# Where DVE's additions of low rows stand among its subtractions, and which engine converts the high part of the experts' activations

## The chip, the cores and the metric

One core of one Trainium2 chip runs the whole kernel in one launch. The time is device microseconds of that core; the kernel before takes 2709.88 us, the median of 3 runs (2704.93 to 2712.09).

## What is computed

Two small transformer stacks, one after the other, on 256 tokens of width 1024 in float32. The first has two layers, each a mixer (attention or a recurrence) followed by a mixture of experts; the second has attention, a long convolution and two dense blocks. The change touches the mixture of experts alone. Cut to what matters:

```python
for g in range(N_GROUPS):          # 4 groups of 8 experts, 2 experts a token
    hid = silu(einsum('nd,edf->nef', x, w_gate[g])) * einsum('nd,edf->nef', x, w_up[g])
    y = y + einsum('nef,efd->nd', hid * combine[:, g, :, None], w_down[g])
```

There are 32 experts a layer. w_gate and w_up are 1024x512 each, w_down is 512x1024: three slabs of 2 MB an expert.

## The kernel before

**Five engines with a program each.** The program is written by hand for every engine, and each engine runs its list strictly in the order in which it is written; they meet at semaphores. So what stands ahead of what on an engine is what the Python code says, and no scheduler changes it. SP issues the loads of weights, 2 MB at a time, into a ring of six slabs. PE multiplies. ACT and DVE do the rest; POOL does little.

**Two parts of every float32 number.** PE multiplies in the format fp32r, which keeps fewer bits. To keep precision, a weight w is split into a high part (w converted to fp32r) and a low part (w minus the high part). ACT makes the high part of half a slab (`make_high`, L1698, 128x2048, into one of four buffers `high`), DVE the low part (`make_low`, L2394, written over the slab in place), and PE multiplies with both. The activations are split as well: `seated2` for the gathered tokens, `hidden2` for the hidden values of an expert, whose high part stands in `hidden2[:, :, 0]` and its low part in `hidden2[:, :, 1]`. The left operand of a matmul holds the high and low parts of 64 tokens side by side in 128 rows, so a bank has 64 rows for the high and 64 for the low part, which have to be added.

**Rounds.** `moe_short` (taken when no expert has more than 64 tokens, as here) runs 16 rounds a layer, one for each pair of experts, 0 and 1. On PE a round is: gate0, up0 (L1126), then down1 of the pair before (L1153), fold0 (L1143), the turn of the routing weights, gate1, up1, the scatter of the pair before (L1174), gathers for the next pair (L1115) with down0 between them, and fold1. Names like down0.1 are expert 0, second half of the slab. Rounds 2 to 14 are one hardware loop; rounds 0, 1 and 15 are written out.

**ACT in a round** (L1739 to L1760): `into` takes one projection's result out of its bank between the two `make_high` of a later slab; `empty_rows` copies the 64 low rows of down's bank to `low_rows`; `silu(e)` and `turn_weights` and `gather` take banks out. A `make_high` may begin when PE is done with the buffer that it overwrites (semaphore `half_used` or the bank's count). The slab that each one prepares is one or two steps ahead: during gate0 it is down1, during up0 gate1, during down1 up1, during gate1 down0, during up1 gate0 of the next round, during down0 up0 of the next round (`next_weights`, L460).

**DVE in a round** (L2424 to L2443): `refill` makes the two low parts of the same slab as ACT's. `add_rows(e, half, r)` adds `low_rows` to the high rows of down's bank and frees that bank (L2421). `hide(e, r)` (L2402) waits for the fold's bank and for silu, multiplies (L2408), casts the product to fp32r as the high part (L2411), waits for that cast, and subtracts for the low part (L2413), which PE's down waits for (semaphore `hidden`). `weigh` (L2380) and `take_seats` (L2372) are four short instructions each, for the routing weights and for the places of the next tokens.

**Banks.** Four PSUM banks carry the round by a fixed table (`FILLS`). PE may fill a bank only when its last content was taken out: gate1's bank holds down1.0 before it, so PE waits there for `add_rows(1, 0)`; up1's holds down1.1; up0's holds down0.1 of the round before; gate0's holds down0.0.

Of the kernel before, what the change touches and what calls it, by code (L numbers as in the profile page):

```python
# [16 lines left out]
F32 = mybir.dt.float32  # L17
# [3 lines left out]
ALU = mybir.AluOpType  # L21
# [308 lines left out]
def build(nc, A, out):  # L330
# [5 lines left out]
    with ctx:  # L336
# [1171 lines left out]
        def _(act):  # L1508
# [177 lines left out]
            def moe_short(layer):  # L1686
# [44 lines left out]

                def gather(j, r):
                    out_of(f"gather{j}", r, seated2[:, 2 * j:2 * j + 2].rearrange("p k e a c -> p (k e a c)"),
                           lambda ps: ps[:, :])

                def turn_weights(r):
                    out_of("turn", r, weightedT, lambda ps: ps[:, 0:2 * P])

                def round_(r, first=False, last=False):  # L1739
                    into("gate0", 0, r, first, last)  # L1740
                    into("up0", 1, r, first, last)
                    if not first:
                        down(1, 0, r, first, last)
                        down(1, 1, r, first, last)
                    silu(0, r)
                    if not first:
                        turn_weights(r)
                    into("gate1", 0, r, first, last)
                    into("up1", 1, r, first, last)
                    if not last:  # L1750
                        gather(0, r)
                        gather(1, r)
                    down(0, 0, r, first, last)
                    if not last:
                        gather(2, r)
                    empty_rows(0, 1, r)
                    if not last:
                        gather(3, r)
                    refill("down0", r, 1, first, last)
                    silu(1, r)  # L1760

# [134 lines left out]
        def _(dve):  # L1896
# [470 lines left out]
            def moe_short(layer):  # L2367
# [20 lines left out]
                def make_low(name, r):  # L2388

                    for half in range(2):  # L2390
                        n, hi = weight_part(name, r, half)
                        w, low = (weight_half(layer, name, half, x) for x in (False, True))
                        dve.wait_ge(sem(f"high{layer}"), n + 1)
                        v.tensor_tensor(low, w, hi.bitcast(F32), ALU.subtract)\  # L2394
                            .then_inc(sem(f"low{layer}"), 1)

                def refill(name, r, first, last):
                    follower = next_weights(name, r, first, last)
                    if follower is not None:
                        make_low(*follower)  # L2400

                def hide(e, r):  # L2402
# [3 lines left out]
                    steps = sem(f"hide_step{layer}")  # L2406
                    h4_, s4 = (x.rearrange("p (f c) -> p f c", f=4) for x in (pair_h, pair_silu))
                    v.tensor_tensor(h4_, s4, ps[:, 4 * SEATS:8 * SEATS].rearrange("p (f c) -> p f c", f=4), ALU.mult)\  # L2408
                        .then_inc(moe_drained[layer][u.bank], 1)
                    moe_empty(dve, layer, u)  # L2410
                    v.tensor_copy(hidden2[:, :, 0], h4_).then_inc(steps, 1)  # L2411
                    dve.wait_ge(steps, r * 2 + (e + 1))
# [11 lines left out]
                def round_(r, first=False, last=False):  # L2424
                    refill("gate0", r, first, last)
                    refill("up0", r, first, last)
                    if not first:
                        add_rows(1, 0, r)
                        add_rows(1, 1, r)
                        refill("down1", r, first, last)  # L2430
# [3 lines left out]
                    weigh(r)  # L2434
                    refill("gate1", r, first, last)
                    refill("up1", r, first, last)
                    add_rows(0, 0, r)
                    add_rows(0, 1, r)
                    refill("down0", r, first, last)
# [3 lines left out]
                    hide(1, r)  # L2443
# [3 lines left out]
                make_low("gate0", 0)  # L2447
                make_low("up0", 0)
# [378 lines left out]
```

## Time and profile before

| | |
|---|---|
| median of 3 runs | 2709.88 us |
| the profiled execution | 2710.59 us |
| its span on the core | 2708.5 us |
| busy: PE, DVE, ACT | 2371.8, 1968.6, 1342.7 us |
| costliest group: the low parts of the experts' weights on DVE (L2394), 384 instructions | 856.6 us |
| next: their high parts on ACT (L1698), 384 instructions | 726.9 us |
| mean granted clock of PE | 0.928 |

A busy time is the sum of an engine's instructions, and a share is that over the whole span, in which stages with different limits follow each other; it tells which engine works most, not which one the others wait for. For that one reads a single stage in order of time, with the idle time before each instruction and what ended it.

### The profile page before, as it was taken

The page shows a single profiled execution, that of the slowest core. Times are in us where ns is not written, and L with a number is a line of the kernel's source. Part 1 is how long each engine was busy: PE and PEld are TensorE (multiplying, and loading weights), DVE is VectorE, ACT ScalarE, POOL GpSimd, SP SyncE. Part 2 cuts the span into 40 slices and gives each one's busy share as a digit, 9 for nine tenths or more (in the row PEclk, how much of TensorE's full clock was granted, in tenths as well). Part 3 has the DMA queues.
Part 4 walks back from the last instruction along what each step waited for, and adds up shares of the span by engine and source line. Part 5 has one row for each costly group of instructions (what it writes and reads, how often), then busy time and mean ns, then how long its engine had stood idle before and what let it go on. Part 6 is the DMA issues. An engine that isn't in the chain of part 4 may idle for free.

```text
span 2708.5 us, 29901 instructions
## 1 busy us (share of the span) xinstructions
PE 2371.8 (88%) x10986; PEld 1749.8 (65%) x10986; DVE 1968.6 (73%) x2443; ACT 1342.7 (50%) x1477; POOL 23.9 (1%) x45
## 2 busy tenths in 40 slices
PE   7996999999998967999999987898799568877998
PEld 6555777777773546777777764565788225733887
DVE  3737999999984548999999985447876644368775
ACT  3225888888872417888888841262432111100432
POOL 0000000000000000000000000000000000000000
PEclk9986999999998988999999997899899678988999
DMA  8313989888993215899989883304656501306370
GB/s 316 124 63 144 367 349 359 355 343 352 353 361 115 112 63 221 348 353 354 362 348 367 354 304 112 124 32 158 231 194 226 212 31 54 133 8 242 140 279 17
DMA packets 116505, 607.80 MB, mean 224 GB/s; under 512 B 5300, under 2 KB 8428, under 8 KB 91644
## 3 DMA queue, kind: packets, MB, share of 16 engines
q1 hardware_dynamic: 111536, 588.83, 56.9%
q0 software_dynamic: 4880, 17.76, 1.8%
q8 instruction: 60, 0.98, 0.2%
q14 instruction: 29, 0.24, 0.0%
HBM read 605.51 MB, written 1.05 MB: 224 GB/s over the span
## 4 chain that ended last, share of the span: by engine, by line
PE 59%; DVE 21%; issue 12%; ACT 7%; DVEq 1%; DMA 0%; POOL 0%; ACTq 0%; SPq 0%
PE bank L900 10%; PE bank L1126 9%; DVE slab_parts L2394 6%; PE bank L912 4%; PE bank L1174 4%; ACT high L1698 3%; PE bank L999 3%; PE bank L1153 3%; PE bank L1387 2%; PE bank L1389 2%; PE bank L1388 2%; PE bank L1400 2%; PE bank L1402 2%; PE bank L1401 2%; PE bank L1115 2%
## 5 line engine op out<-in xcount | busy, mean ns | idle before, releaser
L2394 DVE TENSOR_TENSOR slab_parts<-ring,high 128x2048 fp32r<-128x2048 f32 x384 | 856.6, 2285 | 18.1 <-ACT high L1698 14.2
L1698 ACT ACTIVATE high<-ring 128x2048 fp32r<-128x2048 f32 x384 | 726.9, 1911 | 94.4 <-PE bank L1126 79.9
L1126 PE MATMUL bank<-high,xT_parts 128*128 128x512 f32 x1024 | 291.9, 408 | 34.1 <-DVE arena L2421 32.7
L1126 PE MATMUL bank<-slab_parts,xT_parts 128*128 128x512 f32 x1024 | 282.2, 398 | 0.0
L1538 ACT ACTIVATE arena<-bank 128x512 f32<-128x512 f32 (+4 forms) x162 | 89.5, 586 | 361.2 <-PE bank L900 99.5
L900 PE MATMUL bank<-ring,xT 128*128 128x512 f32 (+3 forms) x576 | 240.5, 579 | 11.1 <-DVE xT L2025 7.1
L1126 PEld LDWEIGHTS bank<-high,xT_parts 128*128 128x128 f32 x1024 | 191.9, 192 | 81.7 <-DVE slab_parts L2394 34.9
L1126 PEld LDWEIGHTS bank<-slab_parts,xT_parts 128*128 128x128 f32 x1024 | 196.3, 192 | 45.8
L1690 ACT ACTIVATE arena<-bank 64x512 f32<-64x512 f32 (+2 forms) x352 | 184.4, 533 | 62.2 <-PE bank L1153 54.6
L900 PEld LDWEIGHTS bank<-ring,xT 128*128 128x128 f32 x576 | 112.1, 196 | 136.3 <-issue 124.7
L1153 PE MATMUL bank<-high,hidden_parts 128*128 128x512 f32 x512 | 151.5, 418 | 18.0 <-DVE slab_parts L2394 11.8
L1558 ACT ACTIVATE high<-ring 128x2048 fp32r<-128x2048 f32 x64 | 121.8, 1913 | 87.8 <-PE bank L1402 82.2
L2606 DVE TENSOR_TENSOR slab_parts<-ring,high 128x2048 fp32r<-128x2048 f32 x64 | 146.1, 2291 | 20.9 <-ACT high L1558 20.5
L1387 PE MATMUL bank<-xT_parts,high 128*128 128x256 f32 x512 | 148.2, 289 | 10.2 <-DVE slab_parts L2606 10.2
L1389 PE MATMUL bank<-xT_parts,slab_parts 128*128 128x256 f32 x512 | 145.7, 285 | 0.0
L1388 PE MATMUL bank<-xT_low,high 128*128 128x256 f32 x512 | 145.6, 284 | 0.0
L2421 DVE TENSOR_TENSOR arena<-arena,bank 64x512 f32<-64x512 f32 x128 | 84.6, 680 | 79.1 <-ACT arena L1690 77.3
L1153 PE MATMUL bank<-slab_parts,hidden_parts 128*128 128x512 f32 x512 | 141.9, 399 | 0.0
L1143 PEld LDWEIGHTS bank<-arena 128*128 128x128 f32 x1024 | 121.8, 192 | 5.9 <-ACT arena L1690 3.1
L1143 PE MATMUL bank<-arena 128*128 128x64 f32 x1024 | 123.0, 273 | 2.3 <-ACT arena L1690 2.3
L1153 PEld LDWEIGHTS bank<-high,hidden_parts 128*128 128x128 f32 x512 | 88.1, 191 | 56.9 <-DVE slab_parts L2394 34.5
L1115 PE MATMUL bank<-sel,u_high 128*128 128x128 f32 x512 | 109.7, 297 | 11.4 <-DVE sel L2372 7.8
(361 smaller groups left out, 3635.9 us busy)
## 6 DMA issues: line engine op xcount, KB each, us to landing
ring<-in_moe_w_gate SPq DMA_DIRECT2D x64, 2048.0 KB, 8.1
ring<-in_moe_w_up SPq DMA_DIRECT2D x64, 2048.0 KB, 10.0
ring<-in_moe_w_down SPq DMA_DIRECT2D x64, 2048.0 KB, 9.0
ring<-in_mlp_w SPq DMA_DIRECT2D x32, 2048.0 KB, 13.6
ring<-in_w_mod SPq DMA_DIRECT2D x24, 2048.0 KB, 7.9
ring<-in_even_w_in SPq DMA_DIRECT2D x7, 2048.0 KB, 21.3
ring<-in_odd_w_in SPq DMA_DIRECT2D x6, 2048.0 KB, 9.6
ring<-in_h_w_in SPq DMA_DIRECT2D x6, 2048.0 KB, 8.2
```

The source lines that it names most:

```text
L900: last = mm(banks[u.bank][:, 0:n], lhs(k, tile), w[:, k, c0:c0 + n], start=(k == 0), stop=(k == k_tiles - 1))
L1115: last = mm(dst5[:, c, :, a], u_parts[a][:, t, 2 * j + c, :], sel[:, t], start=(t == 0), stop=(t == 1))
L1126: last = mm(dst[:, :], seated2[:, 4 * half + k, e], part_[:, k, :], start=(half == a == k == 0), stop=(half == a == 1 and k == 3))
L1143: last = mm(dst[:, (4 * w + f) * SEATS:(4 * w + f + 1) * SEATS], raw[:, w, f * P:(f + 1) * P], fold, start=True, stop=True)
L1153: last = mm(dst[:, :], hidden2[:, f], part_[:, f, :], start=(a == f == 0), stop=(a == 1 and f == 3))
L1387: mm(dst, w_high[:, k, fs], xT_high[:, k, :], start=(k == 0), stop=False)
L1388: mm(dst, w_high[:, k, fs], xT_low[:, k, :], start=False, stop=False)
L1389: last = mm(dst, w_low[:, k, fs], xT_high[:, k, :], start=False, stop=(k == KD - 1))
L1690: act_fn(dst, src(banks[u.bank]), func).then_inc(done or moe_drained[layer][u.bank], 1)
L1698: act_fn(hi, weight_half(layer, name, half), ACT.Copy).then_inc(sem(f"high{layer}"), 1)
L2394: v.tensor_tensor(low, w, hi.bitcast(F32), ALU.subtract)\
L2606: v.tensor_tensor(w_low, loaded, w_high.bitcast(F32), ALU.subtract).then_inc(sem("mlp_low"), 1)
```

## The change

It does two things in `moe_short`, in every round of both layers. On DVE the two additions of an expert's low rows no longer stand next to each other: `make_low` and `refill` are cut into halves (`make_low_after`), and a subtraction of weights stands between the two additions of down1 and another between those of down0. And the high part of the hidden values is no longer a cast on DVE: ACT writes it (`hidden_high`, 128x256, from SBUF to SBUF, when the multiplication has drained the fold's bank), and DVE's last subtraction (`hide_low`) waits for ACT. The multiplication `hide` and `hide_low` are now apart, with `weigh` or `take_seats` between them; `take_seats` comes behind `hide(1)`.

```diff
@@ -1729,6 +1729,11 @@
                 def silu(e, r):
                     out_of(f"fold{e}", r, pair_silu, lambda ps: ps[:, 0:4 * SEATS], ACT.Silu, sem(f"silu{layer}"))
 
+                def hidden_high(e, r):
+                    moe_empty(act, layer, filling(f"fold{e}", r))
+                    act_fn(hidden2[:, :, 0], pair_h.rearrange("p (f c) -> p f c", f=4), ACT.Copy)\
+                        .then_inc(sem(f"hidden_high{layer}"), 1)
+
                 def gather(j, r):
                     out_of(f"gather{j}", r, seated2[:, 2 * j:2 * j + 2].rearrange("p k e a c -> p (k e a c)"),
                            lambda ps: ps[:, :])
@@ -1745,6 +1750,7 @@
                     silu(0, r)
                     if not first:
                         turn_weights(r)
+                    hidden_high(0, r)
                     into("gate1", 0, r, first, last)
                     into("up1", 1, r, first, last)
                     if not last:
@@ -1758,6 +1764,7 @@
                         gather(3, r)
                     refill("down0", r, 1, first, last)
                     silu(1, r)
+                    hidden_high(1, r)
 
                 for name in ("gate0", "up0"):
                     for half in range(2):
@@ -2385,31 +2392,34 @@
                     moe_full(dve, layer, u)
                     return u, banks[u.bank]
 
-                def make_low(name, r):
-
-                    for half in range(2):
-                        n, hi = weight_part(name, r, half)
-                        w, low = (weight_half(layer, name, half, x) for x in (False, True))
-                        dve.wait_ge(sem(f"high{layer}"), n + 1)
-                        v.tensor_tensor(low, w, hi.bitcast(F32), ALU.subtract)\
-                            .then_inc(sem(f"low{layer}"), 1)
-
-                def refill(name, r, first, last):
+                def make_low(name, r, half):
+
+                    n, hi = weight_part(name, r, half)
+                    w, low = (weight_half(layer, name, half, x) for x in (False, True))
+                    dve.wait_ge(sem(f"high{layer}"), n + 1)
+                    v.tensor_tensor(low, w, hi.bitcast(F32), ALU.subtract).then_inc(sem(f"low{layer}"), 1)
+
+                def make_low_after(name, r, half, first, last):
                     follower = next_weights(name, r, first, last)
                     if follower is not None:
-                        make_low(*follower)
+                        make_low(*follower, half)
+
+                def refill(name, r, first, last):
+                    for half in range(2):
+                        make_low_after(name, r, half, first, last)
+
+                h4_, s4 = (x.rearrange("p (f c) -> p f c", f=4) for x in (pair_h, pair_silu))
 
                 def hide(e, r):
 
                     u, ps = filled(f"fold{e}", r)
                     dve.wait_ge(sem(f"silu{layer}"), r * 2 + (e + 1))
-                    steps = sem(f"hide_step{layer}")
-                    h4_, s4 = (x.rearrange("p (f c) -> p f c", f=4) for x in (pair_h, pair_silu))
                     v.tensor_tensor(h4_, s4, ps[:, 4 * SEATS:8 * SEATS].rearrange("p (f c) -> p f c", f=4), ALU.mult)\
                         .then_inc(moe_drained[layer][u.bank], 1)
-                    moe_empty(dve, layer, u)
-                    v.tensor_copy(hidden2[:, :, 0], h4_).then_inc(steps, 1)
-                    dve.wait_ge(steps, r * 2 + (e + 1))
+
+                def hide_low(e, r):
+
+                    dve.wait_ge(sem(f"hidden_high{layer}"), r * 2 + (e + 1))
                     v.tensor_tensor(hidden2[:, :, 1], h4_, hidden2[:, :, 0].bitcast(F32), ALU.subtract)\
                         .then_inc(sem(f"hidden{layer}"), 1)
 
@@ -2423,29 +2433,35 @@
 
                 def round_(r, first=False, last=False):
                     refill("gate0", r, first, last)
-                    refill("up0", r, first, last)
+                    make_low_after("up0", r, 0, first, last)
                     if not first:
                         add_rows(1, 0, r)
+                    make_low_after("up0", r, 1, first, last)
+                    if not first:
                         add_rows(1, 1, r)
                         refill("down1", r, first, last)
                     hide(0, r)
                     if not first:
                         filled("turn", r)
                     weigh(r)
+                    hide_low(0, r)
                     refill("gate1", r, first, last)
                     refill("up1", r, first, last)
                     add_rows(0, 0, r)
+                    make_low_after("down0", r, 0, first, last)
                     add_rows(0, 1, r)
-                    refill("down0", r, first, last)
+                    make_low_after("down0", r, 1, first, last)
+                    hide(1, r)
                     if not last:
                         filled("gather3", r)
                         take_seats(r + 2)
-                    hide(1, r)
+                    hide_low(1, r)
 
                 v.tensor_tensor(fold, ident[:, 0:SEATS], ident[:, SEATS:2 * SEATS], ALU.add)
                 take_seats(0)
-                make_low("gate0", 0)
-                make_low("up0", 0)
+                for name in ("gate0", "up0"):
+                    for half in range(2):
+                        make_low(name, 0, half)
                 filled("gather3", -1)
                 take_seats(1)
                 round_(0, first=True)
```

How the instructions stand now. A name like high2 is the buffer, slab4 the place in the ring; slab4 is up0 of the next round, slab2 down1, slab0 gate1, slab5 down0, slab3 gate0 of the next round, slab1 up1. bank1 and bank2 at the additions are those of down0.0 and down0.1. (A number behind an underscore is the program's own.)

On DVE, the last third of the loop's body, from the first addition of expert 0's rows; before:

```order
L2421 TENSOR_TENSOR arena<-arena,bank1 64x512 [waits low_rows0]
...
L2421 TENSOR_TENSOR arena<-arena,bank2 64x512 [waits low_rows0]
...
L2394 TENSOR_TENSOR slab4_parts_53<-ring,high0_60 128x2048 [waits high0]
...
L2394 TENSOR_TENSOR slab4_parts_53<-ring,high1_61 128x2048 [waits high0]
...
L2372 TENSOR_SCALAR sel_56<-resident,arena 128x64
...
L2408 TENSOR_TENSOR arena<-arena,bank3 128x256 [waits silu0]
L2411 CAST hidden_parts_57<-arena 128x4x64 [waits moe0_bank3_drained]
L2413 TENSOR_TENSOR hidden_parts_57<-arena,hidden_parts_57 128x4x64 [waits hide_step0]
```

and with the change:

```order
L2431 TENSOR_TENSOR arena<-arena,bank1 64x512 [waits low_rows0]
...
L2400 TENSOR_TENSOR slab4_parts_53<-ring,high0_60 128x2048 [waits high0]
...
L2431 TENSOR_TENSOR arena<-arena,bank2 64x512 [waits low_rows0]
...
L2400 TENSOR_TENSOR slab4_parts_53<-ring,high1_61 128x2048 [waits high0]
...
L2417 TENSOR_TENSOR arena<-arena,bank3 128x256 [waits silu0]
...
L2379 TENSOR_SCALAR sel_56<-resident,arena 128x64
...
L2423 TENSOR_TENSOR hidden_parts_57<-arena,hidden_parts_57 128x4x64 [waits hidden_high0]
```

A subtraction stands between the additions, the seats have moved behind the multiplication, the cast is gone, and the last subtraction waits for another engine.

On ACT, the middle of the body, from silu(0) to the first half of up1; before:

```order
L1690 ACTIVATE arena<-bank1 128x256 [waits moe0_bank1_filled]
L1690 ACTIVATE arena<-bank2 128x256 [waits moe0_bank2_filled]
...
L1698 ACTIVATE high0_60<-ring 128x2048 [waits slab5_loaded]
...
L1690 ACTIVATE arena<-bank0 128x512 [waits moe0_bank0_filled]
L1698 ACTIVATE high1_61<-ring 128x2048 [waits moe0_bank0_filled]
```

and with the change:

```order
L1690 ACTIVATE arena<-bank1 128x256 [waits moe0_bank1_filled]
L1690 ACTIVATE arena<-bank2 128x256 [waits moe0_bank2_filled]
L1734 ACTIVATE hidden_parts_57<-arena 128x4x64 [waits moe0_bank1_drained]
...
L1698 ACTIVATE high0_60<-ring 128x2048 [waits slab5_loaded]
...
L1690 ACTIVATE arena<-bank0 128x512 [waits moe0_bank0_filled]
L1698 ACTIVATE high1_61<-ring 128x2048 [waits moe0_bank0_filled]
```

The conversion stands behind the turn's bank and ahead of the high part of down0.0, and waits until DVE has drained bank1.

On ACT, the end of the body and what it goes back to; before:

```order
L1698 ACTIVATE high1_61<-ring 128x2048 [waits moe0_bank2_filled]
L1690 ACTIVATE arena<-bank3 128x256 [waits moe0_bank3_filled]
...
L1769 COMPARE_AND_BRANCH
L1698 ACTIVATE high2_62<-ring 128x2048 [waits slab2_loaded,half_used0]
```

and with the change:

```order
L1698 ACTIVATE high1_61<-ring 128x2048 [waits moe0_bank2_filled]
L1690 ACTIVATE arena<-bank3 128x256 [waits moe0_bank3_filled]
L1734 ACTIVATE hidden_parts_57<-arena 128x4x64 [waits moe0_bank3_drained]
...
L1776 COMPARE_AND_BRANCH
L1698 ACTIVATE high2_62<-ring 128x2048 [waits slab2_loaded,half_used0]
```

The second conversion is the last of the body, ahead of the high part of down1.0. PE's list is the same in both.

## Rows read from the trace of the kernel before

**Rows 1.** The page: span, and busy time of each engine.

```profile
span 2708.5 us, 29901 instructions
...
PE 2371.8 (88%) x10986; PEld 1749.8 (65%) x10986; DVE 1968.6 (73%) x2443; ACT 1342.7 (50%) x1477; POOL 23.9 (1%) x45
```

**Rows 2.** Two windows: length, busy PE, PEld, DVE, ACT, POOL; PE's clock, DMA share, GB/s.

```profile
735.93:771.30 35.37, 33.80 (x172) 26.77 (x172) 32.98 (x30) 29.83 (x28) 0.00 (x0) 1.00 0.90 357
...
309.30:346.00 36.70, 35.23 (x172) 27.78 (x170) 32.85 (x31) 29.85 (x28) 0.00 (x0) 0.95 0.87 344
```

**Rows 3.** Groups by line: instructions | busy us, mean ns | idle before them, what ended it.

```profile
L2394 DVE TENSOR_TENSOR slab_parts<-ring,high 128x2048 fp32r<-128x2048 f32 x384 | 856.6, 2285 | 18.1 <-ACT high L1698 14.2
...
L2421 DVE TENSOR_TENSOR arena<-arena,bank 64x512 f32<-64x512 f32 x128 | 84.6, 680 | 79.1 <-ACT arena L1690 77.3
...
L2380 DVE TENSOR_SCALAR arena<-resident,arena 128x64 f32<-128x64 f32 x128 | 31.3, 308 | 0.0
```

**Rows 4.** DVE in order of time, one round: start, us, instruction, [idle before it].

```profile
742.16 0.30 DVE L2411 CAST hidden_parts<-arena 128x256 fp32r<-128x256 f32 x1
...
742.99 8.90 DVE L2394 TENSOR_TENSOR slab_parts<-ring,high 128x2048 fp32r<-128x2048 f32 x4
751.92 1.28 DVE L2421 TENSOR_TENSOR arena<-arena,bank 64x512 f32<-64x512 f32 x2
753.23 4.50 DVE L2394 TENSOR_TENSOR slab_parts<-ring,high 128x2048 fp32r<-128x2048 f32 x2
757.64 0.42 DVE L2408 TENSOR_TENSOR arena<-arena,bank 128x256 f32<-128x256 f32 x1
...
768.57 0.68 DVE L2421 TENSOR_TENSOR arena<-arena,bank 64x512 f32<-64x512 f32 x1
771.30 0.68 DVE L2421 TENSOR_TENSOR arena<-arena,bank 64x512 f32<-64x512 f32 x1 [2.05 <-ACT arena L1690]
```

**Rows 5.** ACT in order of time, the same round.

```profile
738.22 0.37 ACT L1690 ACTIVATE arena<-bank 128x256 f32<-128x256 f32 x1
739.52 1.92 ACT L1698 ACTIVATE high<-ring 128x2048 fp32r<-128x2048 f32 x1 [0.92 <-PE bank L1126]
...
747.84 0.60 ACT L1690 ACTIVATE arena<-bank 64x512 f32<-64x512 f32 x1
...
752.95 0.66 ACT L1690 ACTIVATE arena<-bank 128x256 f32<-128x256 f32 x2
754.96 1.92 ACT L1698 ACTIVATE high<-ring 128x2048 fp32r<-128x2048 f32 x1 [1.36 <-PE bank L1126]
...
764.69 0.60 ACT L1690 ACTIVATE xT_parts<-bank 128x512 fp32r<-128x512 f32 x1 [1.43 <-PE bank L1115]
765.58 0.60 ACT L1690 ACTIVATE xT_parts<-bank 128x512 fp32r<-128x512 f32 x1 [0.30 <-PE bank L1115]
767.49 0.59 ACT L1690 ACTIVATE arena<-bank 64x512 f32<-64x512 f32 x1 [1.31 <-PE bank L1153]
...
771.79 1.91 ACT L1698 ACTIVATE high<-ring 128x2048 fp32r<-128x2048 f32 x1
```

**Rows 6.** PE in order of time, the same round.

```profile
745.34 1.20 PE L1153 MATMUL bank<-high,hidden_parts 128*128 128x512 f32 x4 [0.40 <-DVE slab_parts L2394]
...
752.73 1.19 PE L1126 MATMUL bank<-high,xT_parts 128*128 128x512 f32 x4 [1.11 <-DVE arena L2421]
...
758.39 1.07 PE L1126 MATMUL bank<-high,xT_parts 128*128 128x512 f32 x4
...
766.36 1.09 PE L1153 MATMUL bank<-slab_parts,hidden_parts 128*128 128x512 f32 x4
```

**Rows 7.** DVE and ACT around ACT's wait before the experts of layer 0.

```profile
228.40 0.15 DVE L2340 COPY arena<-arena 128x1 f32<-128x1 f32 x1
228.91 0.16 DVE L2344 TENSOR_REDUCE arena<-arena 128x1 f32<-128x4 f32 x1 [0.36 <-ACT arena L1680]
...
228.59 0.22 ACT L1680 ACTIVATE arena<-arena 128x16 f32<-128x16 f32 x1 [13.81 <-DVE arena L2340]
```

## The prediction

> **What bounds the kernel now.** The page comes first: in one profiled execution of 2708.5 us PE is busy 88%, DVE 73% and ACT 50% [rows 1]. These shares are averages over stages, and the change touches one stage only, the two expert stages of 16 rounds each. So the second view is the groups by line: the 384 subtractions at L2394 cost DVE 856.6 us with 18.1 us of idle before them, the 128 additions at L2421 have 79.1 us of idle before them, and 77.3 us of that ends with an ACT instruction [rows 3]. The third view is one round by itself. From one addition of low rows to the same one a round later it takes 35.37 us; in that window DVE is busy 32.98 us, PE 33.80, ACT 29.83, the DMA engines 0.90 at 357 GB/s, and PE has its full clock [rows 2].
>
> Then the round in order of time. On DVE everything is back to back except one gap of 2.05 us, between the two additions of down0's rows at 768.57 and 771.30 [rows 4]: ACT has not yet taken those rows out of the bank. On ACT the gaps are before high(down0.0) at 754.96, before the gathers at 764.69 and 765.58, and before the rows at 767.49 (1.43, 0.30 and 1.31 us); each ends with PE [rows 5]. On PE the idle time ends with DVE: 0.40 us before down1 and 1.11 us before gate1, the latter on an addition [rows 6]. So **DVE bounds the round**, with ACT in a loose second place: ACT's start of high(down0.0) does not depend on how late DVE is.
>
> **The change, part by part.**
>
> 1. *Additions between subtractions.* The addition of down0.1's rows moves behind one more subtraction. The subtraction spans 2.2 us (742.99 to 751.92 is 8.93 for four, the last 0.11 longer before an addition), the gap was 2.05 us [rows 4]. Taken alone this removes the gap and costs 0.11 us for each new border between a subtraction and an addition: 0.6 between two additions against 0.71 after an addition, and 2.31 against 2.20 before one. In the first half it puts the addition that PE waits for 2.2 us earlier, which removes PE's 1.11 us.
>
> 2. *Two casts leave DVE.* Each is 0.30 us long and holds its slot for about 0.33 us with what lies between it and the next (742.16) [rows 4]; 0.66 us a round. Parts 1 and 2 together would take DVE's own work and waits to 35.37 - 2.05 - 0.66 + 0.4 = 33.1 us.
>
> 3. *Two conversions enter ACT.* This shape, 128x256 from SBUF, is not in the trace on ACT. The nearest are silu, 128x256 from a bank, 0.37 us (738.22) [rows 5], and the 128x16 and 128x2048 ones, 0.22 and 1.92 us [rows 5, 7], between which a straight line gives 0.42. The next instruction can start some 0.1 us before the end. I take 0.30 us of ACT's time for the first, between 0.28 and 0.42, and 0.4 for the second, since the loop's branch follows it.
> The Trainium skill ("ScalarE: Activation LUTs", Rules for kernel authors) budgets about 0.3 us per ACTIVATE plus 0.83 ns per element, and sends plain elementwise work to VectorE; by that the two would take 0.51 us each, which speaks against the change, and the sum below would be some 6 us higher. The silu row shows 0.37 us for as many elements, so I do not use it.
>
> 4. *The wait that comes with them.* This is the term that decides. The conversion waits for DVE's multiplication, and ACT works in order, so everything behind it waits too: high(down0.0), gate1's bank, high(down0.1) and the rest. Where is DVE then? In the first half its multiplication starts at 757.64, while ACT has finished the turn's bank at about 753.6 and starts high(down0.0) at 754.96 [rows 4, 5]. ACT is now held to 757.64 + 0.42 + 0.04 = 758.1, plus 0.3 for the conversion: high(down0.0) starts 3.4 us later than it did. The hop from DVE to ACT is 0.04 (the copy of 228.40 ends 228.55, ACT starts 228.59) [rows 7]. At the end of the round it is the same: the multiplication comes only after subtraction up0.1, which itself waits for the high part that ACT made just before. ACT used to start high(down1.0) at 739.52, 1.2 us after high(up0.1) had ended (773.70, less a round, is 738.33) [rows 2, 5]; now it stands still for a subtraction and a multiplication, 2.7 us. DVE's own wait for the conversion costs nothing: four short instructions, 0.31 us each where they weigh [rows 3], stand between the multiplication and the subtraction that needs it, and hop, conversion and hop are 0.5 us.
>
> So two engines that ran side by side are **tied into a ring**. One turn of it, with each leg from a row:
> - ACT makes high(down1.0), 1.92, and the hop to DVE, 0.04: 1.96 us.
> - DVE goes from that subtraction to the end of the multiplication of expert 0: 742.99 to 758.06 before, without a gap, 15.07 [rows 4]. The new order has one more border pair, +0.22. The first addition of down1's rows now comes three subtractions in, 8.7 us after the start of high(down1.0), and ACT has those rows out 8.91 us after it (739.52 to 748.43) [rows 5]: with the hop +0.3. 15.6 us.
> - Hop and conversion: 0.04 + 0.30.
> - ACT goes from high(down0.0) to the end of high(up0.1): 754.96 to 773.70, less its three waits for PE of 3.04, which are gone because ACT now comes later: 15.7 us [rows 5]. Does PE keep ahead? It can start the second half of up1 when DVE starts that multiplication, and has down0.0 done 758.39 to 767.45, 9.1 us later [rows 6]; ACT comes to its rows 10.3 us later. It does, by 1 us. Hop 0.04.
> - DVE: the subtraction, 2.20, and the multiplication, 0.42: 2.62 us. Hop and conversion: 0.04 + 0.4.
>
> The ring takes 1.96 + 15.6 + 0.34 + 15.74 + 2.62 + 0.44 = 36.7 us; with 0.3 for both conversions 36.6. **I take 36.6**, 1.25 us more than 35.37. The gap that part 1 closes and the casts of part 2 stood beside this ring, on DVE, and buy nothing: DVE now waits for high parts, about 1.1 us at down1.0, 0.9 at down0.0, and 0.5 to 0.7 at each half of up0. The late first addition is in the ring at +0.3.
>
> 32 rounds at 1.25 us make 40 us. One credit: in four rounds, two a layer, PE's clock falls to half for a moment and they take about 36.8 us (309.30 to 346.00, clock 0.95) [rows 2]. PE now stands off the ring with about 1 us to spare, so about 1 us of each is hidden: -4. DMA costs nothing: no transfer or its release moves, and a longer round asks for less than the 357 GB/s of now. PE's instructions are the same.
>
> The sum: the profiled execution took 2710.6 us (span 2708.5 and 2.1 around it), 0.7 above the median of the three runs, 2709.9. 2710.6 + 40 - 4 - 0.7 = 2746 us.
>
> The bounds: the conversions at 0.28 and 0.42 give -3 and +6 us over 64 of them; the hops, seen at 0.04 and 0.10 (ACT ends 228.81, DVE starts 228.91) [rows 7], up to +8 over four hops; the clock credit between 0 and -6; the ring leg on DVE without the 0.3 and 0.22, -17.
>
> **The rivals.**
>
> *A, faster: the relief arrives.* If ACT's wait were hidden, the round would fall to the next bound, PE: 35.37 less its 1.51 us of waits, 33.9 us, 32 x 1.5 = 47 us less, 2663 us. For it: DVE is the engine that is full, and its gap and casts are really gone. The Trainium skill ("Perfetto Trace Analysis", Identifying the Most-Contended Engine) says to relieve the engine with the highest occupancy first, and to judge PE by its weight loads rather than by its matmuls: by it DVE, 32.98 of 35.37 against 26.77 for the weight loads, is the one, and the change is right. Against: it needs DVE's multiplication to be over before ACT comes, and it ends over 4 us later, at a place where DVE has no slack to run ahead, since each of its subtractions needs a high part of ACT's. Chance 6%.
>
> *B, no change.* The ring lies between 35.3 and 35.5 us, because DVE's leg is shorter than I think and ACT overlaps better at its waits. It needs 1.2 us off my sum, and the terms without a row are together 0.5. 2710 us, chance 4%.
>
> *C, slower by more.* PE loses its spare 1 us in the second half and enters the ring: then ACT waits at the rows of down0 as well, and the half-clock moments count fully. The point from which it decides is 1 us of delay on PE between up1 and down0. Priced as the ring plus one such wait of 0.7 us: 32 x 1.95 = 62 us, 2772. Chance 10%.
>
> *D, the change does not do what it says.* Where DVE's and ACT's instructions stand is as the diff says in both loops, so all that is left is that the first and last rounds differ. No chance of its own.
>
> **How the numbers follow.** My forecast, the ring at 36.1 to 37.0 us a round, has 80%; A 6, B 4, C 10. The predicted time is the forecast's. Its own bounds are 2710.6 + 32 x 0.7 - 6 = 2727 and 2710.6 + 32 x 1.65 + 0 = 2763. To hold 8 in 10 with A, B and part of C outside, I widen to 2722 and 2768. A measurement of this kernel tells about 0.3%, 8 us, from no change. Faster by more than that: A and a little of B, 0.06. Within: 0.05. Slower: 0.89.
>
> **What would show it.** In the profile after: a round of 36.6 us; on ACT, idle time before the new conversions that ends with DVE, about 3.5 us at the first and 2.4 at the second in each round, some 180 us over 64; ACT's waits for PE before the gathers gone; DVE's idle before the additions (79 us) mostly gone, but new idle before the subtractions of weights (L2400 in the new file), ended by ACT, of some 3 us a round, 100 us in all; PE's wait for an addition replaced by waits for subtractions and, at fold1, for ACT. Wrong would be: a round under 35.4 us, or ACT reaching the conversion after DVE's multiplication.

## The result, and the profile after

| | before | after |
|---|---|---|
| median of 4 runs each, us | 2707.4 (2704.63 to 2712.09) | 2741.5 (2736.76 to 2746.51) |
| span of the profiled execution, us | 2708.5 | 2738.6 |
| one round in the steady part of layer 1 / layer 2, us | 35.37 / 35.37 | 36.43 / 36.50 |
| both expert stages, us | 1167.7 | 1200.7 |

The change makes the kernel slower: the ratio after to before is 1.0124, with a 95% interval of 1.0099 to 1.0149. An expert stage is counted from the last cast of its routing (`most_tokens`) to the start of the last addition of its output; the two are 33.0 us longer, and the rest of the span is 2.9 us shorter, in code that is the same. That rest is 3.8 us shorter ahead of the first stage, 3.7 longer between the two and 2.8 shorter behind the second, and PE's mean granted clock goes with it: 0.91 before and 0.93 after, 0.87 and 0.83, 0.89 and 0.90. Why the clock differs in the same code is open.

The page after, the rows that answer to [rows 1]:

```profile
span 2738.6 us, 29901 instructions
...
PE 2382.7 (87%) x10986; PEld 1746.9 (64%) x10986; DVE 1960.9 (72%) x2379; ACT 1356.5 (50%) x1541; POOL 23.9 (1%) x45
```

DVE has 64 instructions fewer and is busy 7.7 us less, ACT has 64 more and is busy 13.8 us more. (The casts were 64 times 0.30, 19 us. Part of that comes back, since subtractions that stand apart overlap less: the same 384 are busy 867.4 us, below, and were 856.6.) Both shares hardly move. By this view alone the change is a good trade, since the fuller engine is relieved. The loss is in no busy time; it is in the waits.

One round of each layer (the columns are those of [rows 2]):

```profile
745.08:781.51 36.43, 34.32 (x172) 26.68 (x172) 32.73 (x28) 30.31 (x30) 0.00 (x0) 1.00 0.87 345
1558.10:1594.60 36.50, 34.33 (x172) 26.68 (x172) 32.72 (x29) 30.32 (x30) 0.00 (x0) 1.00 0.88 346
```

DVE was idle or between instructions for 2.39 us of a round (35.37 less 32.98), and is now for 3.70. DMA's share is down. PE has its full clock and stands still for 2.02 us of the round, 1.51 before: 0.93, 0.15 and 0.65 us until a subtraction of DVE is done, and 0.29 us for ACT. So neither of them is the new limit.

The groups by line, as in [rows 3]:

```profile
L2400 DVE TENSOR_TENSOR slab_parts<-ring,high 128x2048 fp32r<-128x2048 f32 x384 | 867.4, 2290 | 118.7 <-ACT high L1698 116.8
...
L2431 DVE TENSOR_TENSOR arena<-arena,bank 64x512 f32<-64x512 f32 x128 | 87.1, 682 | 22.9 <-ACT arena L1690 20.0
...
L1734 ACT ACTIVATE hidden_parts<-arena 128x256 fp32r<-128x256 f32 x64 | 26.8, 418 | 182.8 <-DVE arena L2417 182.8
```

What the first part of the change was for is there: the additions' idle time fell from 79.1 to 22.9 us. Two new waits have come: 182.8 us of ACT standing before the new conversions, all of it ended by DVE's multiplication, and 118.7 us (18.1 before) of DVE standing before its subtractions, nearly all ended by ACT. DVE waits for ACT, which waits for DVE.

ACT in order of time through one round, to be held against [rows 5]; the conversion at 749.08 is that of expert 1, at the loop's end, the one at 767.04 that of expert 0:

```profile
749.08 0.42 ACT L1734 ACTIVATE hidden_parts<-arena 128x256 fp32r<-128x256 f32 x1 [2.42 <-DVE arena L2417]
749.49 1.92 ACT L1698 ACTIVATE high<-ring 128x2048 fp32r<-128x2048 f32 x1
...
767.04 0.42 ACT L1734 ACTIVATE hidden_parts<-arena 128x256 fp32r<-128x256 f32 x1 [3.46 <-DVE arena L2417]
767.36 1.90 ACT L1698 ACTIVATE high<-ring 128x2048 fp32r<-128x2048 f32 x1
...
775.53 1.07 ACT L1690 ACTIVATE xT_parts<-bank 128x512 fp32r<-128x512 f32 x2
776.62 0.59 ACT L1690 ACTIVATE arena<-bank 64x512 f32<-64x512 f32 x1
...
780.91 1.91 ACT L1698 ACTIVATE high<-ring 128x2048 fp32r<-128x2048 f32 x1
```

The waits for PE that stood before the gathers and the rows (1.43, 0.30 and 1.31 us) are gone, and in their place stand 2.42 and 3.46 us before the conversions. DVE in the same round, against [rows 4]:

```profile
748.63 0.41 DVE L2417 TENSOR_TENSOR arena<-arena,bank 128x256 f32<-128x256 f32 x1
...
751.43 6.78 DVE L2400 TENSOR_TENSOR slab_parts<-ring,high 128x2048 fp32r<-128x2048 f32 x3 [1.40 <-ACT high L1698]
758.43 0.68 DVE L2431 TENSOR_TENSOR arena<-arena,bank 64x512 f32<-64x512 f32 x1 [0.21 <-ACT arena L1690]
...
766.59 0.41 DVE L2417 TENSOR_TENSOR arena<-arena,bank 128x256 f32<-128x256 f32 x1
...
769.29 8.98 DVE L2400 TENSOR_TENSOR slab_parts<-ring,high 128x2048 fp32r<-128x2048 f32 x4 [1.07 <-ACT high L1698]
778.30 0.68 DVE L2431 TENSOR_TENSOR arena<-arena,bank 64x512 f32<-64x512 f32 x1
779.19 2.29 DVE L2400 TENSOR_TENSOR slab_parts<-ring,high 128x2048 fp32r<-128x2048 f32 x1 [0.21 <-ACT high L1698]
781.51 0.68 DVE L2431 TENSOR_TENSOR arena<-arena,bank 64x512 f32<-64x512 f32 x1
782.85 2.29 DVE L2400 TENSOR_TENSOR slab_parts<-ring,high 128x2048 fp32r<-128x2048 f32 x1 [0.66 <-ACT high L1698]
```

The gap of 2.05 us between the additions of down0 is closed (778.30 and 781.51 have a subtraction between them), but there are 3.55 us of waits for high parts and rows elsewhere (1.40, 0.21, 1.07, 0.21 and 0.66). One causes the other: the high part that DVE lacks at 751.43 is the one that ACT began at 749.49, because it stood from 746.66 on for DVE's multiplication of 748.63.

### The profile page after: what moved, and what is told of

It reads as the page before. It is cut to its first block, busy times and chain, and to the rows that moved or that the text cites. A ratio compares the mean times of both kernels' runs of the same rounds, so it can differ in the third digit from the quotient of the medians.

```text
span 2738.6 us, 29901 instructions
## 1 busy us (share of the span) xinstructions
PE 2382.7 (87%) x10986; PEld 1746.9 (64%) x10986; DVE 1960.9 (72%) x2379; ACT 1356.5 (50%) x1541; POOL 23.9 (1%) x45
## 4 chain that ended last, share of the span: by engine, by line
PE 50%; DVE 19%; ACT 19%; issue 10%; DVEq 1%; DMA 0%; ACTq 0%; POOL 0%; SPq 0%
ACT high L1698 11%; PE bank L900 10%; PE bank L1126 6%; DVE slab_parts L2400 6%; PE bank L912 4%; ACT arena L1690 4%; PE bank L999 3%; PE bank L1387 2%; PE bank L1389 2%; PE bank L1388 2%; PE bank L1400 2%; PE bank L1402 2%; PE bank L1401 2%; ACT xT_parts L1690 2%; PE bank L1143 2%
## 5 line engine op out<-in xcount | busy, mean ns | idle before, releaser
L2400 DVE TENSOR_TENSOR slab_parts<-ring,high 128x2048 fp32r<-128x2048 f32 x384 | 867.4, 2290 | 118.7 <-ACT high L1698 116.8
L1126 PEld LDWEIGHTS bank<-high,xT_parts 128*128 128x128 f32 x1024 | 185.2, 191 | 84.2 <-DVE slab_parts L2400 43.2
L2622 DVE TENSOR_TENSOR slab_parts<-ring,high 128x2048 fp32r<-128x2048 f32 x64 | 146.1, 2291 | 20.9 <-ACT high L1558 20.6
L1174 PE MATMUL bank<-arena 128*128 128x512 f32 x256 | 115.2, 593 | 2.7 <-DVE arena L2431 2.7
```

Of the source, the lines that this page charges most:

```text
L1126: last = mm(dst[:, :], seated2[:, 4 * half + k, e], part_[:, k, :], start=(half == a == k == 0), stop=(half == a == 1 and k == 3))
L2400: v.tensor_tensor(low, w, hi.bitcast(F32), ALU.subtract).then_inc(sem(f"low{layer}"), 1)
L2622: v.tensor_tensor(w_low, loaded, w_high.bitcast(F32), ALU.subtract).then_inc(sem("mlp_low"), 1)
```

## The experiments

The two parts of the change were first taken apart, then the joint between the engines was cut into its wait and its work, then each place was tried alone. Diffs are against the changed kernel. Rounds are those of the steady loop in layer 1.

### The additions alone (e1_rows_only)

The cast goes back to DVE; `hidden_high` does nothing, and `hide` does all four steps again, behind `take_seats`.

```diff
 def hidden_high(e, r):
-    moe_empty(act, layer, filling(f"fold{e}", r))
-    act_fn(hidden2[:, :, 0], pair_h.rearrange("p (f c) -> p f c", f=4), ACT.Copy)...
+    pass
...
+    v.tensor_copy(hidden2[:, :, 0], h4_).then_inc(steps, 1)
```

> Only the additions are moved; the high part of the hidden values is cast by DVE again, as before, and ACT waits for nothing new. Theory W (ACT's new wait for DVE's multiplication is the whole loss, and the moved additions by themselves help): the gap of 2.05 us before the second addition goes, 34.5 us a round against 35.37, about 26 us less than before, 2681 us; what is left on DVE is a wait of about 0.7 us for the high part of up0.1. Rival O (the additions between subtractions are what hurts, because DVE now meets ACT's high parts just as they are made): slower than before, 36 us a round or more, 2730 us.

Measured: 2677.8 us, ratio to before 0.9885 (0.9860 to 0.9909). One round:

```profile
714.00:748.64 34.64, 34.04 (x171) 26.58 (x171) 33.24 (x31) 29.83 (x28) 0.00 (x0) 1.00 0.89 364
```

The additions between subtractions are worth 0.73 us a round and 1.1% of the kernel. So the first half of the change is not worthless: it gains about 30 us, and with the second half the kernel is some 64 us slower than without it (2741.5 against 2677.8).

### The conversions alone (e2_act_only)

The additions stand together again; ACT keeps the conversions.

```diff
-make_low_after("up0", r, 0, first, last)
+refill("up0", r, first, last)
 if not first:
     add_rows(1, 0, r)
-make_low_after("up0", r, 1, first, last)
...
```

> Only the conversions move to ACT; the two additions of an expert stand next to each other again. W: the ring is the same, 36.6 to 36.7 us a round, 2745 us, as slow as the whole change or a little slower, ACT idle about 3.5 us before the first conversion of a round and 2.4 us before the second. O: as fast as before or faster, 35.4 us a round or less, 2705 us.

Measured: 2750.8 us, ratio 1.0147 (1.0122 to 1.0171); the round is 36.52 us, against 36.43 with both parts. ACT stands 3.05 us before the first conversion of a round and 2.91 before the second, where 3.5 and 2.4 were expected. Its group of conversions:

```profile
L1734 ACT ACTIVATE hidden_parts<-arena 128x256 fp32r<-128x256 f32 x64 | 26.8, 418 | 184.6 <-DVE arena L2417 184.6
```

With the conversions on ACT, the additions' place makes 0.09 us; without them it makes 0.73. The conversions set the round, whatever DVE has gained.

### The wait without the work (e5_wait_only)

ACT waits for the multiplication where it did, but converts nothing; DVE casts.

```diff
 moe_empty(act, layer, filling(f"fold{e}", r))
-act_fn(hidden2[:, :, 0], ...)...
```

> The additions are moved, DVE casts the high part itself as before, and ACT does no conversion but waits at the same two places for the same multiplications. W: the wait alone makes the loss, about 36.6 us a round, 2745 us. Rival L (the conversions' own time on ACT, 0.42 us each, 64 of them, is what costs): without them the round is that of the moved additions alone, 34.5 us, 2681 us.

Measured: 2747.7 us, ratio 1.0137 (1.0113 to 1.0161), a round of 36.92 us. ACT's instruction behind each bare wait:

```profile
720.30 1.92 ACT L1698 ACTIVATE high<-ring 128x2048 fp32r<-128x2048 f32 x1 [3.46 <-DVE arena L2415]
738.00 1.92 ACT L1698 ACTIVATE high<-ring 128x2048 fp32r<-128x2048 f32 x1 [3.61 <-DVE arena L2415]
```

The wait alone, with DVE's casts untouched, costs all of the loss. It costs even 0.49 us a round more than the changed kernel. The seats, 0.65 us of DVE from start to start, stand ahead of the multiplication here, and so in the ring. Against that, the first conversion is missing; but its place was only 0.36 us with the hop, and the bare wait takes 0.19: DVE's multiplication ends at 737.81, and ACT starts at 738.00. 0.65 less 0.17 is 0.48. At the loop's end nothing is saved: from the end of the multiplication (719.86) to ACT's start (720.30) it is 0.44 us without the conversion and 0.45 with it.

### The work without the wait (e6_work_only)

ACT does 64 conversions of the same shape at the same places, from constants into a place that nobody reads.

```diff
-moe_empty(act, layer, filling(f"fold{e}", r))
-act_fn(hidden2[:, :, 0], pair_h...)...
+act_fn(spare, resident[:, P:3 * P].rearrange("p (f c) -> p f c", f=4), ACT.Copy)
```

> The additions are moved, DVE casts the high part itself as before, and ACT does a conversion of the same shape at the same two places, of constants and into a place that nobody reads, without any wait. W: ACT has idle time to hide it in, 34.5 us a round, 2681 us, the same as with the moved additions alone. L: the 0.3 to 0.4 us of each show, 0.7 us a round or more, 35.2 us a round, 2704 us or above.

Measured: 2676.9 us, ratio 0.9882 (0.9856 to 0.9907), and a round of 34.65 us, as without them.

```profile
L1734 ACT ACTIVATE spare<-resident 128x256 fp32r<-128x256 f32 x64 | 26.8, 418 | 0.0
```

Exactly the same busy time on ACT, 26.8 us, costs nothing when it waits for nothing. This pair settles the question: ACT's wait for DVE makes the loss, not ACT's work.

### One place at a time (e3_down0_rows, e4_down1_rows)

Both have the cast on DVE. The first puts a subtraction between the additions of down0 alone, the second between those of down1 alone.

```diff
 # e3: down1's additions together
-make_low_after("up0", r, 0, first, last)
+refill("up0", r, first, last)
...
 # e4: down0's additions together
-make_low_after("down0", r, 0, first, last)
-make_low_after("down0", r, 1, first, last)
+refill("down0", r, first, last)
```

> Of the moved additions only those of down0 (the later half of a round); DVE casts, no conversion on ACT. If the gap before the second addition is what the move buys: the gap of 2.05 us goes, but DVE still waits about 0.7 us for the high part of up0.1, and the addition that gate1 waits for on PE stays where it was: 34.9 us a round, 2693 us. If both halves are needed: 35.4, 2707.

> Of the moved additions only those of down1 (the first half of a round). PE's wait of 1.1 us before gate1 goes, so PE and with it ACT's low rows of down0.1 are earlier, and DVE's gap before the second addition shrinks by a part of that: 35.0 us a round, 2695 us. If PE's wait does not matter because DVE bounds the round: 35.4 or a little more (one more border between addition and subtraction, 0.1 us), 2708 us.

Measured: down0 alone 2699.7 us, 0.9972 (0.9958 to 0.9985), a round of 34.87; down1 alone 2694.6 us, 0.9958 (0.9942 to 0.9974), a round of 35.13. In rounds they are additive: 0.50 and 0.24 make the 0.73 of both. In time they are not: by the medians, the one whose round is longer is the faster kernel, though single runs of the two overlap (2692.8 to 2702.8 us, and 2692.7 to 2698.8). Two neighbouring rounds of the first show why:

```profile
697.44:732.31 34.87, 33.69 (x173) 26.76 (x171) 33.06 (x30) 29.83 (x28) 0.00 (x0) 1.00 0.91 360
732.31:768.72 36.41, 35.23 (x173) 27.90 (x171) 33.06 (x30) 29.82 (x28) 0.00 (x0) 0.95 0.88 345
```

Nine of its rounds, five in layer 1 and four in layer 2, hold a moment at half clock, which costs 1.54 us each (36.41 less 34.87); down1 alone has none. Nine times 1.54 is 14 of the 22 us that lie between it and the kernel with both places, and 32 rounds at 0.23 are another 7.

### The first conversion later, and one joint alone (e7_later_conversion, e9_one_joint_cut)

The seventh experiment moves ACT's first conversion behind the first high part of down0 and gate1's bank, and DVE's subtraction for it behind the two of down0. The ninth has that, and gives the second conversion back to DVE, whose multiplication of expert 1 then stands behind the seats, as in e1.

```diff
+refill("gate1", r, 0, first, last)
+out_of("gate1", r, raw[:, 0, :]...)
 hidden_high(0, r)
-into("gate1", 0, r, first, last)
+refill("gate1", r, 1, first, last)
 # e9 as well
 silu(1, r)
-hidden_high(1, r)
```

> The whole change, with one thing put elsewhere: ACT's conversion of expert 0 stands behind gate1's bank instead of ahead of the high part of down0.0, and DVE's subtraction for it behind the two of down0. The same instructions. W: at that place DVE's multiplication is nearly over when ACT comes, so the idle time before it falls from 3.5 us to some 0.5, and the ring is cut at one of its two joints: 35.7 us a round, 2717 us. If the place does not matter: 36.4, 2741.

> As with the later conversion of expert 0 (35.8 us a round, 2715 us), but expert 1's high part is cast by DVE again, so ACT no longer waits for DVE at the end of the round; expert 0's stays on ACT at its later place. W, a ring that needs both joints: with the one at the end gone, ACT runs ahead again, reaches the remaining conversion after the multiplication or nearly so, and the round falls to that of the moved additions alone, 34.5 to 34.7 us, 2678 us, although 32 conversions are still on ACT and still wait. If instead the remaining wait costs by itself, or ACT's own load does: 35.2 or more, 2700 us.

Measured: the later conversion takes 2715.2 us, 1.0034 (1.0019 to 1.0049), with a round of 35.77; with one joint cut it is 2678.1 us, 0.9885 (0.9867 to 0.9903), with a round of 34.64. ACT in the first, the two conversions and the low rows of down0.0 between them:

```profile
723.58 0.42 ACT L1734 ACTIVATE hidden_parts<-arena 128x256 fp32r<-128x256 f32 x1 [1.17 <-DVE arena L2420]
...
732.51 0.59 ACT L1690 ACTIVATE arena<-bank 64x512 f32<-64x512 f32 x1 [1.31 <-PE bank L1153]
...
741.41 0.42 ACT L1734 ACTIVATE hidden_parts<-arena 128x256 fp32r<-128x256 f32 x1 [2.42 <-DVE arena L2420]
```

The idle time before the first conversion is 1.17 us, more than the 0.5 expected, but it does not set the round: ACT waits for PE behind it, 1.31 us before those rows. PE in turn has stood 0.64 us for a subtraction of DVE's, and has its scatter, gathers and down0.0 still to do. So the chain goes from DVE over PE to ACT, and closes by way of the joint at the loop's end, where ACT still stands 2.42 us. With that joint alone on the chain the round is 1.13 us longer than without it, in the ninth (35.77 against 34.64).

In the ninth, the conversion that is left, and the group:

```profile
743.96 0.42 ACT L1734 ACTIVATE hidden_parts<-arena 128x256 fp32r<-128x256 f32 x1 [1.93 <-DVE arena L2419]
```

```profile
L1734 ACT ACTIVATE hidden_parts<-arena 128x256 fp32r<-128x256 f32 x32 | 13.4, 418 | 57.7 <-DVE arena L2419 57.7
```

In the ninth ACT still stands 1.9 us in a steady round before its conversion, and the kernel is as fast as with no conversion on ACT at all. A wait of that length is harmless here, because ACT is ahead of its work: in the same round it still waits for PE 0.92 us before high(down1.0) and 1.32 before the rows of down0.0, as in e1 (0.93 and 1.31). So it is not that a loss needs both joints. With both on the chain the round is 36.43 us, with the one at the loop's end and PE in place of the other 35.77, and with that one gone 34.64. The first conversion at its old place, with the second on DVE, was not tried, so it is not shown that the first joint alone is harmless there.

### The seats in the wait that is left (e8_seats_early)

With the cast on DVE, DVE in e1 still waits 0.34 and 0.66 us for ACT's high parts, before the two subtractions that it makes during down0. The four instructions of `take_seats`, 0.74 us, can stand ahead of the second of these.

```diff
 add_rows(0, 1, r)
-make_low_after("down0", r, 1, first, last)
-hide(1, r)
 if not last:
     filled("gather3", r)
     take_seats(r + 2)
-hide_low(1, r)
+make_low_after("down0", r, 1, first, last)
+hide(1, r)
```

> The moved additions without the conversions, and DVE's four instructions for the seats put ahead of the last subtraction of a round, up0.1, where it waited 0.66 us for ACT's high part. W: they fill that wait, DVE's round becomes 33.9 us and PE's own work of 33.8 us is the next bound: 33.9 us a round against 34.5, 2660 us, faster than both kernels by 45 and 80 us. If PE, ACT or DMA (0.90 busy before, 0.94 then) already bounds the round at 34.5: 2678 us.

Measured: 2664.0 us (2662.5 to 2667.0), ratio 0.9847 (0.9822 to 0.9871), the fastest of all. Its round, and the one wait that DVE keeps:

```profile
713.99:748.01 34.02, 33.59 (x173) 26.72 (x171) 33.25 (x31) 29.74 (x28) 0.00 (x0) 1.00 0.91 370
```

```profile
745.68 2.29 DVE L2398 TENSOR_TENSOR slab_parts<-ring,high 128x2048 fp32r<-128x2048 f32 x1 [0.34 <-ACT high L1698]
```

The seats have filled the second wait, and the round is 0.62 us shorter. PE is busy 33.59 and DVE 33.25 of its 34.02 us.

## Why the prediction was right

**The ring (part 4) decides, and its legs are as forecast.** Leg by leg from the rows after, high(down1.0) starting at 749.49:

- High part and hop: 751.43 less 749.49, 1.94 (forecast 1.96).
- DVE to the end of the multiplication of expert 0: 751.43 to 767.00, 15.57 (15.6).
- Hop and conversion: 767.00 to 767.36, 0.36 (0.34).
- ACT from high(down0.0) at 767.36 to the subtraction at 782.85: 15.49 (15.74 with the hop).
- That subtraction and the multiplication: 2.62 (2.62).
- Hop and second conversion: 0.45 (0.44), read at the start of the round, 748.63 + 0.41 to 749.49.

They add up to 36.43; the forecast took 36.6. The ACT leg is where it was too long: instructions that no longer wait for PE overlap, as the two gathers show, 1.07 us together where they were 0.60 each and apart (0.13 of the 0.25).

**The price of the conversion (part 3) was right.** It is 0.42 us long, which is the straight line between the two shapes, and ACT's next instruction starts 0.32 us after its start (767.04, 767.36), or 0.41 at the loop's end. The 0.51 us that the prediction worked out from the Trainium skill ("ScalarE: Activation LUTs", Rules for kernel authors) is too much here; the Trainium skill gives that budget for an ACTIVATE whose bias is a [128,1] pointer, and the conversion names no bias. The same page of the Trainium skill states under "What ACT_TABLE_LOAD costs" that an ACTIVATE with immediate scale and bias takes 186 ns + 0.833 ns per element, and that back-to-back ones overlap by about 93 ns. For 256 elements that is an estimate of 0.40 us, and of 0.31 us to the next one. The trace agrees with these: 0.418 us is the mean of the 64, and 0.32 us the distance. None of it matters to the sum as work, as e6 shows. In the bounds the conversions were mis-added: 0.28 and 0.42 us, against the 0.30 and 0.40 of the sum, make 4 us less and 4 more over 32 rounds, not 3 and 6.

**The waits stood where they were forecast.** ACT's idle time before the conversions: 3.46 and 2.42 us, 182.8 in all (forecast 3.5, 2.4, 180). DVE's before the additions is 22.9 us (mostly gone), before the subtractions 118.7 (100 forecast). ACT's waits before the gathers are gone. PE waits for subtractions, and 0.29 us at fold1 for ACT.

**Parts 1 and 2 gain nothing in this kernel**, though e1 shows that part 1 gains 0.73 us a round by itself. The prediction said that they stand beside the ring. For part 1 e2 shows it, with a round longer by 0.09 us only. For part 2 e5 does, where DVE has its casts back and all but 0.01 of the 0.49 us a round is the seats and the hop. What the prediction did not work out is that the second half of the change then costs more than the whole: 64 us against the version without it, where the whole change costs 34.

**Two terms were mis-sized and one was left out.** The ring was put at 40 us over 32 rounds and gives 35 (1.06 us a round in layer 1, 1.13 in layer 2). The clock credit was put at 4 us, four moments of which 1 us each is hidden. After, there is none in the steady rounds of either layer, and in before each cost 1.3 to 1.5 us: the credit is about 6. 35 less 6 makes 29; the stages are 33.0 longer. The other 4 us lie in the last round of each layer, which is written out and was taken as equal to the others: from the multiplication of expert 1 in round 14 to that in round 15 it takes 30.94 us (785.06 to 816.00), and 28.00 before, 2.94 longer and not 1.1. These errors cancel in part, 5 and 2 us one way and 4 the other; that much of the closeness is luck.

**The rivals.** A fell. What fell with it is not the rule of the Trainium skill ("Perfetto Trace Analysis", Identifying the Most-Contended Engine), which says to optimize the engine with the highest occupancy first, but its reading as: take work off that engine. DVE was the fullest engine, and moving work off it made the kernel slower, while e1 and e8, which leave DVE's work as it was and shorten its waits by another order, gain 1.1% and 1.5%. B fell with the round of 36.43. C did not come, but was near: ACT has no wait for PE at the rows of down0, and PE's last matmuls of down0.0, below, end 0.68 us before ACT takes those rows at 776.62, where 1 us was forecast. D fell too, since every row stands as the diff says. PE in order of time, after:

```profile
774.85 1.09 PE L1153 MATMUL bank<-slab_parts,hidden_parts 128*128 128x512 f32 x4
```

## What to carry to other kernels

A small step that goes from a full engine to one with time to spare also carries a wait with it, and an in-order engine makes everything behind the step wait too. Before such a move, look at when the giving engine reaches the producer and when the taking engine reaches the step, and follow the chain, over a third engine too (as over PE in e7), to see whether it comes back; if it does, add its legs and hold the sum against the round. Here the hand-over of two casts, 0.66 us of DVE, cost 1.8 us a round (36.43 against 34.64), while moving 0.7 us of work into a wait that was there anyway gained 0.6.

## What the runs showed of the hardware beyond this

**PE's clock.** The half-clock moments do not go with how long PE stands still in a round. The changed kernel's PE waits 2.0 us a round and has none in its steady rounds; the kernel before waited 1.5 us and had four; e2 had seven and e3 nine. These three (before, e2 and e3) are the ones in which the additions of down1 stand together and PE stands 1.11 us before gate1. e1, e4, e5, e6, e7, e8 and e9 have no such pause, and no such moment. The place in the kernel before, PE in order of time and then the granted clock of the stretch behind it:

```profile
322.02 1.89 PE L1143 MATMUL bank<-arena 128*128 128x64 f32 x16
323.75 0.39 PE L1161 MATMUL bank<-resident,arena 128*128 128x128 f32 x2
325.25 1.65 PE L1126 MATMUL bank<-high,xT_parts 128*128 128x512 f32 x4 [1.11 <-DVE arena L2421]
326.70 1.91 PE L1126 MATMUL bank<-slab_parts,xT_parts 128*128 128x512 f32 x4
```

```profile
325.25:328.20 2.95, 2.95 (x8) 2.34 (x9) 2.92 (x3) 0.96 (x3) 0.00 (x0) 0.59 1.01 433
```

PE did the 16 small matmuls of fold0 and the turn, stood for 1.11 us, and the granted clock fell from 2.4 to 1.2 GHz right behind (0.59 of the full clock on average over these 2.95 us). The pause occurs in every round of these kernels and the fall in few, so it is not the whole cause. One profile of each kernel was read; that the pause belongs to it is a correlation over eleven kernels, not shown by an experiment on the pause alone.

**The second layer's ring** is 0.07 us longer than the first's (36.50 against 36.43), and so it is, by 0.06 to 0.08, in the other kernels in which ACT waits at the loop's end (e2, e5, e7) and in no other. It lies at the loop's end: from the second conversion to high(down1.0) it takes 0.42 us in layer 1 and 0.49 in layer 2 (712.64 to 713.06, 1525.58 to 1526.07). Why it takes longer in the second loop was not tried.
